# Two k-tiles at a time in the ungated products of a decoder trunk in float32

## The reference

```python
def reference(x, mem, ...):
    for i in range(DEPTH):                                    # 2 layers
        h = rmsnorm(x, norm_g[i, 0])
        # mixer: h @ w_in; memory: rmsnorm(mem) @ w_mem_kv[i]
        attn = jnp.concatenate([o_mix, o_mem], axis=-1) @ w_o[i]
        x = x + rmsnorm(attn, norm_g[i, 1])
        h = rmsnorm(x, norm_g[i, 2])
        f = conv_ffn(h, w_ffn_gate[i], w_ffn_up[i], ffn_conv_w[i], ffn_conv_b[i], w_ffn_down[i])
        x = x + rmsnorm(f, norm_g[i, 3])
    return x

def conv_ffn(h, w_gate, w_up, conv_w, conv_b, w_down):
    g_pre = h @ w_gate
    ...
    return (jax.nn.silu(gc) * (h @ w_up)) @ w_down
```

## Time and profile before

| | |
|---|---|
| median of 3 executions | 2437.48 us |
| lowest and highest | 2425.14 and 2438.07 us |
| profiled execution, first to last instruction | 2423.1 us |
| TensorE matmul busy | 2328.8 us, 96% |
| TensorE weight load busy | 2023.2 us, 83% |
| VectorE busy | 1616.9 us, 67% |
| ScalarE busy | 1325.5 us, 55% |
| GpSimd busy | 285.1 us, 12% |
| mean granted TensorE clock | 0.987 of full |

### The profile page before, as it was taken

How to read it: one execution, slowest core, us unless ns; L and a number is a source line. 1 busy time by engine, 2 the same in 40 slices (tenths; PEclk the granted TensorE clock), 3 DMA queues, 4 the chain that set the end, 5 groups by cost and what they waited for, 6 DMA issues and landing times.

```text
span 2423.1 us, 41087 instructions
## 1 busy us (share of the span) xinstructions
PE 2328.8 (96%) x13346; PEld 2023.2 (83%) x13346; DVE 1616.9 (67%) x2422; ACT 1325.5 (55%) x1861; POOL 285.1 (12%) x316
## 2 busy tenths in 40 slices
PE   7999999979999999999979999997999999999996
PEld 6888888868888888888868888886888888888885
DVE  5666655777777777655567778767776777765555
ACT  5555554466666666544345544346666666653332
POOL 0000000210000000000034233221000000000001
PEclk9999999989999999999989999998999999999998
DMA  6544444535555555655544643353555565565553
GB/s 228 182 156 157 165 164 143 187 114 181 196 184 191 189 188 193 189 190 185 189 157 157 210 143 100 105 190 105 185 191 178 188 193 174 191 190 185 183 183 124
DMA packets 118040, 418.13 MB, mean 173 GB/s; under 512 B 13264, under 2 KB 13520, under 8 KB 117984
## 3 DMA queue, kind: packets, MB, share of 16 engines
q1 hardware_dynamic: 116784, 413.62, 52.3%
q10 hardware_dynamic: 720, 2.18, 0.3%
q0 software_dynamic: 480, 1.60, 0.2%
HBM read 414.20 MB, written 3.15 MB: 172 GB/s over the span
## 4 chain that ended last, share of the span: by engine, by line
PE 91%; DVE 5%; ACT 2%; DMA 1%; POOL 1%; issue 1%; DVEq 0%; SPq 0%; ACTq 0%; POOLq 0%
PE gemm L771 55%; PE gemm L773 28%; PE gemm L823 2%; PE SB L610 1%; PE OB L603 1%; PE SA L603 1%; DVE lo L1059 1%; PE gemm L825 1%; DVE x L1216 1%; DVE y L1210 1%; ACT hi L867 1%; PE SB L603 1%; DMA raw<-in_cmp 0%; DMA raw<-in_mem 0%; DVE rpost L1207 0%
## 5 line engine op out<-in xcount | busy, mean ns | idle before, releaser
L771 PE MATMUL gemm<-h,hi 128*128 128x512 f32 x3824 | 1351.8, 398 | 3.3 <-DVE lo L1059 2.5
L1059 DVE TENSOR_TENSOR lo<-raw,hi 128x1024 fp32r<-128x1024 f32 (+1 forms) x794 | 974.1, 1247 | 378.4 <-ACT hi L867 370.6
L773 PE MATMUL gemm<-h,lo 128*128 128x256 f32 x3824 | 1067.8, 279 | 0.0
L867 ACT ACTIVATE hi<-raw 128x1024 fp32r<-128x1024 f32 (+1 forms) x794 | 788.3, 1034 | 184.5 <-PE gemm L773 172.8
L771 PEld LDWEIGHTS gemm<-h,hi 128*128 128x128 f32 x3824 | 717.9, 188 | 175.3 <-DVE lo L1059 2.6
L773 PEld LDWEIGHTS gemm<-h,lo 128*128 128x128 f32 x3824 | 720.7, 188 | 0.6
L878 ACT ACTIVATE cross<-gemm 128x256 f32<-128x256 f32 x325 | 124.5, 383 | 749.5 <-PE gemm L773 740.0
L771 PE MATMUL gemm<-mid,hi 128*128 128x512 f32 x1408 | 494.4, 393 | 0.0
L773 PE MATMUL gemm<-mid,lo 128*128 128x256 f32 x1408 | 398.2, 283 | 0.0
L771 PEld LDWEIGHTS gemm<-mid,hi 128*128 128x128 f32 x1408 | 264.5, 188 | 61.1
L773 PEld LDWEIGHTS gemm<-mid,lo 128*128 128x128 f32 x1408 | 264.7, 188 | 0.0
(11 more groups left out here) (222 smaller groups left out, 1835.9 us busy)
## 6 DMA issues: line engine op xcount, KB each, us to landing
raw<-in_ffn SPq DMA_DIRECT2D x352, 512.0 KB, 4.2
raw<-in_in SPq DMA_DIRECT2D x138, 512.0 KB, 4.0
raw<-in_down SPq DMA_DIRECT2D x128, 448.0 KB, 4.0
raw<-in_out SPq DMA_DIRECT2D x64, 512.0 KB, 4.0
raw<-in_down SPq DMA_DIRECT2D x64, 512.0 KB, 3.9
raw<-in_mem SPq DMA_DIRECT2D x32, 512.0 KB, 4.7
raw<-in_cmp SPq DMA_DIRECT2D x16, 512.0 KB, 4.7
memT<-in_memT SPq DMA_DIRECT2D x4, 512.0 KB, 9.4
```

Source lines behind the costliest of these rows:

```text
L771: mm(out[:, 0:2 * T], hi[slot][:, at:at + P], act[:, kt, :, :].rearrange("p a t -> p (a t)"), start=k == 0, stop=False, skip_group_check=True)
L773: m = mm(out[:, T:2 * T], lo[slot][:, at:at + P], act[:, kt, 0, :], start=False, stop=k == sum(s.pieces) - 1, skip_group_check=True)
L867: act(hi[k][:, 0:kt * P], raw[k][:, 0:kt * P], ACT.Copy).then_inc(hi_done, 1)
L1059: tt(lo[k][:, 0:kt * P], raw[k][:, 0:kt * P], hi[k][:, 0:kt * P].bitcast(F32), ALU.subtract)\
```

## The change

In `gemm`, a slot without a gate now handles a piece with an even number of k-tiles two at a time: both 512-column matmuls with `hi`, then both 256-column matmuls with `lo`. Pieces of 7 k-tiles, gated slots, `gemm_pair` and `compress` stay as they are. The wait at the head of a piece and the signal with its last matmul stay where they are.

```diff
                 for j, kts in enumerate(s.pieces):
                     pe_.wait_ge(lo_done, s.n(i, j + 1))
+                    at_kt = k
+                    if not s.gate and kts % 2 == 0:
+                        slot = s.n.slot(j)
+                        for two in range(0, kts, 2):
+                            for kt in (k, k + 1):
+                                at = (kt - at_kt) * P
+                                mm(out[:, 0:2 * T], hi[slot][:, at:at + P], act[:, kt, :, :].rearrange("p a t -> p (a t)"),
+                                   start=kt == 0, stop=False, skip_group_check=True)
+                            for kt in (k, k + 1):
+                                at = (kt - at_kt) * P
+                                m = mm(out[:, T:2 * T], lo[slot][:, at:at + P], act[:, kt, 0, :],
+                                       start=False, stop=kt == sum(s.pieces) - 1, skip_group_check=True)
+                            k += 2
+                        m.then_inc(piece_done, 1)
+                        continue
                     for _ in range(kts):
```

## The result

| | kernel before | kernel after |
|---|---|---|
| median of 9 executions | 2437.47 us | 2422.2 us |
| lowest and highest | 2425.14 and 2442.5 us | 2416.88 and 2425.5 us |
| span of the profiled execution | 2423.1 us | 2420.4 us |

The ratio is 0.9949, with a 95% interval of 0.9931 to 0.9967: the kernel became faster by 0.5%, some 12 us, with 8 and 17 us as the ends. Two things in the table belong together. The medians differ by 15 us, the spans of the two profiled executions by 3. And the kernel before spreads over 17 us, the kernel after over 9.

A forecast was written before the change was run, and what follows sets the result against it. The prediction took TensorE's own matmul spacing as the bound. Reordering added zero to the profiled span of 2423.1 us; with the 14.4 us up to the median this gave 2437 us, range 2405 to 2465 us.

The forecast's parts named there:

- The bound: Whole kernel: TensorE, busy 96% of the span, paces the products itself; time is k-tiles times the spacing of two matmuls.
- Own width: Changed pairs: each spacing goes by the matmul's own width, 0.2325 and 0.1175 us, 0.700 us a pair in both orders; 0.66.
- The loads: Second short matmul in a row: its weight load stays hidden, 0.093 us against 0.117 us, at a value of nothing.
- 24 ns to spare: Weight loads behind 256-column matmuls: the margin left when a load follows a load after 0.093 us and a matmul leaves 0.117.
- the slow rival: Changed pairs: two short matmuls in a row outrun the loads, 20 ns x 2472 = 49 us slower, 2487 us; chance 0.14.
- The cadence: 4944 changed k-tiles: all in the fastest cadence (346.2 ns) saves 19 us, all in the slowest (353.0) costs 15 us.
- the sum of zero: Whole change: 4944 reordered k-tiles cost the same in both orders, about 0.350 us each, so the span changes by 0.
- The base: Starting time: profiled span 2423.1 us plus the 14.4 us by which it stands under the median, giving 2437 us.
- Changeover: Fast rival, changed pairs: excess is paid where width changes; half the changeovers go, 74 us or 31 us faster; chance 0.20.
- the fast rival: Changed pairs: excess is a price of changing over, 2363 us or 2407 us; VectorE and ScalarE about 265 us in 350; 0.20.
- the case within the forecast in which the cadence carries it past half a percent: Changed k-tiles: spacing by own width, but the cadence makes the kernel over 0.5% (12 us) faster; 0.08 of the 0.66.

## Why the prediction was right or wrong

**The bound, right.** TensorE's spacing sets the time, and the whole difference lies in the windows of its matmuls. No wait came or went.

**Own width, right in its use and wrong in its reason.** The two spacings that no row showed came out as taken: 0.23 us for 512 after 512, 0.115 for 256 after 256, against 0.2325 and 0.1175. But I had reasoned that the excess goes with the columns, 10 ns on 256 and 19 on 512, by the compression. With 128-column loads and 256 columns throughout it is 13.3 ns a matmul where it reads `h`, 360 ns for three, and 12 where it reads `mid`. The compression differs in its loads (30 columns) and in its operands' addresses; which of the two makes its 10 ns is not shown. Two excesses of 13.3 ns are 346.7 ns for a k-tile, which is the fast cadence. The rest of the old order's 350 comes from the cadence.

The prediction says that the gap which the Trainium skill, "TensorE: Matmul & The Clock Gate", section "Back-to-back issue gap", gives, 325 ns for a k-tile, confirms that the gap goes by the own width. It can't: that section gives the formula for a matmul by itself, and says that it doesn't hold for a stream of loads and matmuls, which this is. No window here gave less than 346 ns.

**The loads, right in the outcome, wrong in the margin.** Eight short ones in a row held. But the 24 ns to spare, from 0.093 us for a load behind a load in the earlier trace rows, were a misreading: the three spacings of that row are not alike. In two short windows on the same row (144.17 to 144.25 and 144.39 to 144.41 us):

```profile
144.10 0.20 PEld L664 LDWEIGHTS TA<-cst,pm 128*128 128x128 f32 x2 [0.85 <-DVEq L1259]
144.27 0.25 PEld L664 LDWEIGHTS TA<-cst,pm 128*128 128x128 f32 x2
```

With 0.14 us for one load, the second starts 0.06 us after the first, the fourth 0.11 us after the third. The single starts are 58, 112 and 109 ns apart, and in all eight such rows the last two spacings are 109 to 112 ns. So in these rows a load behind a load takes some 109 ns, and a short matmul of 117 ns leaves 8 to spare. That is the 107 ns and the 10 to spare which the prediction takes from the Trainium skill, "TensorE: Matmul & The Clock Gate", section "LDWEIGHTS (loading the stationary operand)", and sets aside for its own 24; the trace agrees with the page. That the slow rival, given 0.14 on the wrong margin, stayed away was in part luck.

**The cadence, seen and mis-sized.** The prediction named it and gave 2418 to 2452 us for it. The time came out inside the range, and the step that was off is the sum of zero. It set the cadence of the new order equal to the old one's mean, 350.0 ns, and there was no reason for that: the new order has its own, 348.1 ns in both layers. On the gate and up projections this is 2 ns worse than the fast cadence and 5 ns better than the slow one. The profiles of the kernels with these products in the old order at distance 0 show them slow in 5 of 8 cases (four profiles, two layers each), 350.4 ns on average; 2752 k-tiles x 2.4 ns are 7 us, and their experiment measured 7 us (3 to 11). The groups of the 74 executions give the same: 1.35 slow layers on average are 12 us over none, and the new order gives 4 of them back (1.6 ns on 2752 k-tiles), which leaves 8 us. The rest of the change measured 4 us, not told apart from zero. Together 11 us, against the 12 of the whole; the intervals are wide, and the sum can't be held to a microsecond.

**The base, wrong.** I took the 14.4 us between span and median for what lies around the span. In the nine executions of the kernel after each time is 1.8 us above its span (2422.24 and 2420.4 in the profiled one). So the first profile was of an execution of about 2425 us, one of the faster ones of the kernel before, with one slow layer and little time at the low clock. The median, 2437 us, stood for others: of the 74 executions above, all of 2436 us or more are in the group that fits two slow layers. I had one layer fast and one slow in front of me in the earlier trace rows, and should have asked which of them is usual. Sums against that span would still have said zero. And the two profiles hide part of the gain: their spans differ by 3 us, their products of span and clock (2392 and 2384) by some 7, since the profiled execution of the kernel after spent more time at the lower level.

**The rivals.** Changeover, at 0.20, is refuted three times: four at a time is slower than two, eight isn't faster, and with no changes at all an excess of 12 to 13 ns stays on each matmul. The slow rival, at 0.14, is refuted, as it was priced, by eight at a time. (In the sum of the fast rival ScalarE would come to 249 us in 350, not 265; nothing hangs on it.) The measured gain came by neither, but by the case within the forecast in which the cadence carries it past half a percent, to which I gave 0.08; the interval of the ratio, 0.3 to 0.7% faster, has that bound inside it.

## What to carry to other kernels

Where TensorE is the bound, read the time of a k-tile from counts in long windows of each product, and compare loops of the same code: if they differ, the stream has more than one steady cadence. An order that has only one takes away spread, and it gains what the usual case lies above that one cadence. Here, reordering matmuls whose loads are hidden took no price off them; it selected a cadence, and so did moving an operand by 64 or 128 bytes against the weights, which costs less to try. Read the rate of a row of instructions from its single starts and not from its ends, since the first spacing can be another. And before a sum is set against a span, see whether the profiled execution was a usual one: span times mean granted clock, over many executions, shows the groups.

## What the runs showed of the hardware

- A stream of matmuls with identical instructions and addresses ran at 346.2 ns per k-tile in some executions and at 352.8 in others (layer 0 of the first profile and of the kernel with everything else changed), and kept either through a stretch of 350 us. What chooses is open. Layer 1 was slow in the two profiles of the kernel before and fast in one in which only `o`, `mid` and `amem1` lay elsewhere; and span times clock of 74 executions of one program falls into three groups 8 to 9 us apart, which fit none, one and two slow layers, so it seems to change from one execution to the next.
- The cadences depend on the distance of moving operand and weights in SBUF: in the old order 0 bytes gave 346 or 353 ns and 128 gave 350 to 351; in the new order 0 gave 348 and 64 gave 346. Each shifted layout ran in one execution. Why was not found. A weight load starts within 0.01 us of a matmul's start, so a conflict of the two reads is a possible reason, but no run here shows it.
- In a stream of 256-column matmuls with a load of 128 columns behind each, a matmul cost 13.3 ns over its columns at 2.4 GHz where it reads `h` (360 ns for three, 0.12 us apart) and 12 ns where it reads `mid` (355.7 ns for three). Eight of 512 columns in a row stood 0.231 us apart, 18 ns over 213.
- Four float32 loads of 128 columns in a row (line 664 of the kernel before) started 58, 112 and 109 ns apart; the last two spacings were 109 to 112 ns in all eight such rows.
- The same kernel, with the same cadences, took 8.5 us longer in one execution than in another, with the lower clock in more of its stages with gaps (0.94 against 0.89 in one window of 30 us).
